# Eighteen additions and subtractions on VectorE, moved one by one between blocks of matmuls

## The reference

```
ua = einsum(ya * silu(ga), w_up_a);  ub, uc in the same way
gates = sigmoid(gm)                  # gm = h @ w_in[:, GM:], 3 x 1024 columns
merged = gates[0] * ua + gates[1] * ub + gates[2] * uc
x = x + merged @ w_o
```

## Time and profile before

| | |
|---|---|
| time, median of 3 runs | 1227.82 us (1226.7 to 1228.06) |
| profiled execution, its own time | 1227.92 us |
| its span from first to last instruction | 1225.8 us |
| PE busy | 1209.8 us, 99% of the span |
| DVE, ACT, POOL busy | 58%, 50%, 58% of the span |
| mean granted clock of TensorE | 0.997 of full speed |

### The profile page before, as it was taken

How to read it: one execution, slowest core, us unless ns; L and a number is a source line. 1 busy time by engine, 2 the same in 40 slices (tenths; PEclk the granted TensorE clock), 3 DMA queues, 4 the chain that set the end, 5 groups by cost and what they waited for, 6 DMA issues and landing times.

```text
span 1225.8 us, 18317 instructions
## 1 busy us (share of the span) xinstructions
PE 1209.8 (99%) x6667; PEld 991.0 (81%) x6667; DVE 711.2 (58%) x1235; ACT 607.9 (50%) x1176; POOL 705.5 (58%) x538
## 2 busy tenths in 40 slices
PE   9999999999998999999999999999999999999997
PEld 7987777787876899987897777878888888889886
DVE  5554427757657777745597555434454445966224
ACT  6365535676633344455645665544444444333544
POOL 8673233263368776856384557446555655886842
PEclk9999999999999999999999999999999999999999
DMA  6332222222222333354142123333333332334332
GB/s 240 106 88 85 60 64 58 60 70 73 59 70 77 95 104 95 105 188 112 52 118 61 46 73 88 103 86 96 92 89 104 96 89 82 103 92 120 107 86 69
DMA packets 62432, 112.22 MB, mean 92 GB/s; under 512 B 6856, under 2 KB 11464, under 8 KB 62344
## 3 DMA queue, kind: packets, MB, share of 16 engines
q1 hardware_dynamic: 62200, 111.06, 31.7%
q10 hardware_dynamic: 144, 0.00, 0.0%
HBM read 108.87 MB, written 2.16 MB: 91 GB/s over the span
## 4 chain that ended last, share of the span: by engine, by line
PE 91%; DVE 5%; ACT 1%; POOL 1%; issue 1%; DMA 0%; SPq 0%; DVEq 0%; POOLq 0%; ACTq 0%
PE pb L1093 22%; PE pb L1094 22%; PE pb L1096 21%; PE pb L1146 3%; PE pb L1148 3%; PE pb L1147 3%; PE pb L1302 2%; DVE t7s L2034 2%; PE pb L1278 2%; PE pb L1155 2%; PE pb L1245 1%; PE pb L1216 1%; PE pb L1218 1%; PE pb L1217 1%; PE pb L1199 1%; PE pb L1197 1%
## 5 line engine op out<-in xcount | busy, mean ns | idle before, releaser
L2650 POOL TENSOR_TENSOR wlo<-raw,whi 128x512 fp32r<-128x512 f32 (+2 forms) x384 | 522.1, 1379 | 331.0 <-ACT whi L1495 330.0
L1093 PE MATMUL pb<-HH,whi 128*128 128x512 f32 x856 | 345.6, 404 | 1.0 <-DVE th L1971 1.0
L1094 PE MATMUL pb<-HL,whi 128*128 128x512 f32 x856 | 338.5, 395 | 0.0
L1096 PE MATMUL pb<-HH,wlo 128*128 128x512 f32 x856 | 337.5, 394 | 0.0
L1495 ACT ACTIVATE whi<-raw 128x512 fp32r<-128x512 f32 (+2 forms) x384 | 226.0, 615 | 105.1 <-PE pb L1096 54.7
L1093 PEld LDWEIGHTS pb<-HH,whi 128*128 128x128 f32 x856 | 161.3, 188 | 43.6 <-issue 4.6
L1094 PEld LDWEIGHTS pb<-HL,whi 128*128 128x128 f32 x856 | 161.1, 188 | 38.0 <-issue 2.9
L1096 PEld LDWEIGHTS pb<-HH,wlo 128*128 128x128 f32 x856 | 160.9, 188 | 37.5
L1959 DVE TENSOR_TENSOR pb<-pb,rff 128x512 f32<-128x512 f32 x44 | 30.8, 700 | 124.0 <-PE pb L1096 117.6
L1604 ACT ACTIVATE P<-P,stat 128x256 f32<-128x256 f32 (+3 forms) x96 | 50.6, 528 | 78.5 <-DVE stat L2212 56.1
L2650 POOL TENSOR_TENSOR fl<-cv,fh 128x512 fp32r<-128x512 f32 x22 | 28.9, 1315 | 86.4 <-ACT fh L1880 86.4
(11 more groups left out here) (459 smaller groups left out, 2526.0 us busy)
## 6 DMA issues: line engine op xcount, KB each, us to landing
raw<-in_wall SPq DMA_DIRECT2D x368, 256.0 KB, 2.8
raw<-in_wall SPq DMA_DIRECT2D x8, 260.0 KB, 3.0
X<-in_xT SPq DMA_DIRECT2D x8, 256.0 KB, 5.1
X<-in_xT SPq DMA_DIRECT2D x2, 1024.0 KB, 7.4
outT<-PP SPq DMA_DIRECT2D x8, 256.0 KB, 2.4
raw<-in_wall SPq DMA_DIRECT2D x10, 192.0 KB, 2.4
raw<-in_wall SPq DMA_DIRECT2D x9, 128.0 KB, 2.5
cst<-in_cst SPq DMA_DIRECT2D x1, 832.0 KB, 7.3
```

The costliest lines, as they stand in the source:

```text
L1093: pe.do.matmul(b, hi, xh[k], start=start, stop=False, skip_group_check=tile[0] == "down")
L1094: pe.do.matmul(b, hi, xl[k], start=False, stop=False, skip_group_check=tile[0] == "down")
L1096: m = pe.do.matmul(b, lo, xh[k], start=False, stop=stop, skip_group_check=tile[0] == "down")
L2650: g.do.tensor_tensor(lo, x, hi.bitcast(F32), ALU.subtract).then_inc(*up(name, point))
```

## The change

Sets 0, 1 and 2 are no longer issued as runs. Their single instructions (`t_piece`, i = 0 to 5) and then the set's `t_parts` go into a list, `extra`, from which `slot` takes one at blocks 1 and 5 of a tile. Set 0 is put in ahead of the gate tiles of C, set 1 ahead of the early `gm` tiles, set 2 after gate tile B0. The 18 DVE instructions, 3 of ACT and 6 of POOL are the same ones as before, in other places; PE and SP keep their rows. `t_sums` stays for set 3 and for the second block.

```diff
@@ slot
     def slot(self, i):
         if i in (3, 7):
             self.step()
+        elif i in (1, 5) and self.extra:
+            self.add(*self.extra.pop(0))
@@ stages
+        def pieces(kp):
+            self.extra += [("t_piece", kp, i) for i in range(6)] + [("t_parts", 0, kp)]
+
+        pieces(0)
         for t in range(4):
             gate("gateC", "yC", t)
+        pieces(1)
         add("masks_in")
         for d in range(3):
             for j in range(3):
                 gm(d, j)
         for t in range(4):
             gate("gateA", "yA", t)
-            if t in (1, 3):
-                add("t_sums", 0, t // 2)
-            if t == 2:
-                add("t_parts", 0, 0)
         for t in range(4):
             gate("gateB", "yB", t)
-            if t < 2:
-                add(("t_parts", "t_sums")[t], 0, 1 + t)
+            if t == 0:
+                pieces(2)
         while self.background:
             self.step()
-        add("t_parts", 0, 2)
+        while self.extra:
+            add(*self.extra.pop(0))
@@ vector
+            def t_piece(kp, i):
+                x11, x12, x21, x22 = (TS7[kp][:, H * n:H * n + H] for n in range(4))
+                v.wait_ge(*at("values", *[("C", 7, 3), ("A", 3, 3), ("B", 7, 3)][kp:kp + 1]))
+                if kp == 2:
+                    v.wait_ge(*at("yA", 3))
+                if i < 2:
+                    n = kp + 4 * i
+                    v.wait_ge(*at("x_lo", n))
+                    v.wait_ge(*at("x_hi", n))
+                    dst, one, two, op = TS7[kp][:, T * i:T * i + T], hh[n].bitcast(F32), hl[n].bitcast(F32), ALU.add
+                else:
+                    v.wait_ge(*last("v_t7"))
+                    dst, one, two = ((x11, x12, x11), (x12, x22, x12), (x22, x22, x11), (x21, x21, x22))[i - 2]
+                    op = ALU.subtract
+                v.do.tensor_tensor(dst, one, two, op).then_inc(*up("v_t7", *[("t_raw", 0, kp)] * (i == 5)))
```

More of the change, by code:

```diff
@@ L192, in __init__ @@
         self.slot_of, self.slot_user, self.slot_before, self.slots = {}, {}, {}, 0
+        self.extra = []
         self.background, self.heads, self.gates, self.ticks = [], [], [], 0
@@ L2633, in half_out @@
                         mul(PP[d][:, c], PP[d][:, c], r, ("final", d, half))
-            follow({"begin": begin, "split": split, "t_sums": t_sums, "product7": product7, "first": first, "square": square,
+            follow({"begin": begin, "split": split, "t_piece": t_piece, "t_sums": t_sums, "product7": product7, "first": first, "square": square,
                     "lambda": lam_dots, "norm1": norm1, "kC_out": kc_out,
```

## The result

The changed kernel takes 1230.08 us (median of 11 runs, 1229.48 to 1231.03), the kernel before 1227.62 (11 runs beside it, 1226.47 to 1228.25). The ratio is 1.0025 with a 95% interval of 1.0017 to 1.0032: a loss of 2.5 us where 1.05 was forecast. The profiled execution has a span of 1227.8 us, 2.0 more than before.

What follows compares the result with a forecast made beforehand. PE bounds the kernel, working 1209.8 of 1225.8 us. Added 0.68 + 0.5 + 3.7 + 1.57 = 6.45 us, taken away 5.40, so 1227.82 + 1.05 = 1228.9 us; range 1223.4 to 1231.0 us, forecast's own 1227.5 to 1230.3.

Steps and rivals of the forecast that it cites:

- What is taken away: Gates of B: PE's waits for th (1.17 us) and yBlo (2.66) and the slow clock (1.57) go, 5.40 us.
- C0 and C1: Gate tiles of C: pieces ahead of score reads make PE wait, 0.68 us in C0 and 0.5 in C1.
- The third gm tile: PE waits 3.7 us for a late read of B's scores, then loses 1.57 us to a slow clock.
- The 1.0 us by which A's last head ends late: Before the third gm tile: ACT's splitting of set 0 (0.3) and set 0's pieces delay A's end 1.0 us.
- The two pieces ahead of the first read: Set 1's pieces before B's first score read, both at the high price beside POOL: 3.18 us, less 0.85 idleness.
- The pieces ahead of the second read: Set 1's next two pieces, before the score read at 280.95: 1.8 us, less 1.42 of DVE idleness.
- The clock: After the long wait at the third gm tile PE's clock falls to 0.50, losing 1.57 us.
- the rule on POOL: POOL holds up DVE instructions with two SBUF inputs or in 2-port mode; every piece exposed, bank reads not.
- Hidden pieces: Rival: pieces mostly run alone, costing 1.1 us, so 4.3 us are gained: 1223.5 us; chance 0.20.
- A wait without the slow clock: Rival: DVE 1 to 3 us late at the second B step, PE stays at 2.4 GHz: 1225.8 us; chance 0.22.
- The other side: Rival: at the second B step PE waits 5.4 us and the clock falls, 3.05 lost: 1230.9 us; chance 0.12.
- the change doesn't do what it says: Rival: B's gates are late for another reason, only the 1.17 us wait goes: 1233.1 us; chance 0.04.

Runs made afterwards that it cites:

- set 1 alone: Against the kernel before, only set 1 taken apart into pieces, ahead of the gm tiles; sets 0 and 2 stay whole runs behind A1 and B1: 1225.29 us, ratio 0.9984.
- set 0 alone: Against the kernel before, only set 0 taken apart into pieces, in C; sets 1 and 2 stay whole runs behind A3 and B1: 1225.27 us, ratio 0.9984.
- parts of set 0 later: Against the changed kernel, the parts of set 0 (ACT's t7h, two t7l on POOL) come behind gate tile A1 instead of C3: 1227.76 us.
- the last kernel: Against the kernel before, only the parts of set 0 moved, behind the last gate of B in place of A2: 1225.88 us, ratio 0.9987.

## Why the prediction was right, and where its sizes were off

**What is taken away: right, 5.6 us against 5.40.** Both waits and the slow clock are gone, and the kernel with all pieces behind gates shows that the sum can be had whole. But the reason given, that the set in front of each gate makes it late, was too narrow. With set 0 or set 1 alone out of the row, runs remain ahead of B0 or B2 and make next to no wait (0.3 us), and with all three runs in place the wait for `th` goes when the parts of set 0 are moved. In these kernels a run makes little or no wait where the gate ahead of it is in time; runs and their parts in a row pass their delays on. That did not enter the sum, since the change takes all three away.

**C0 and C1: 0.57 + 0.71 = 1.28 us against 0.68 + 0.5 = 1.18.** Both are near the reckoning. The piece in C0 ran alone, the one in C1 beside POOL's `wlo` took 1.79.

**The third gm tile: the term that was too small.** The wait was put at 3.7 us and the clock at 1.57, 5.27 together; they took 6.28. That PE would wait here for a score read, and that the clock would fall, came as forecast; the terms from which the size of the wait was summed don't hold one by one:

- The 1.0 us by which A's last head ends late is right: 272.71 - 270.42 is 2.29, less PE's own 1.28. But ACT's `t7h`, for which the prediction counted 0.3 of it, has no share. With the parts of set 0 moved away the lateness is the same, and with set 1 alone there is none (`qA` starts 10.67 us ahead of the transposes, as before); it is the pieces of set 0 themselves.
- The two pieces ahead of the first read took 2.05 + 1.40 = 3.45 us against 3.18. They would have been dear without set 0 as well (1.77 + 1.44 with set 1 alone).
- Not in the sum at all: the masks `B`, two DVE instructions that were there before. The prediction cost `t7l`'s delay of POOL's `wlo` at nothing, because the weights are split ahead; PE indeed waits for no `wlo` from C0 on. But a later `wlo` falls on other DVE work: the pair of masks took 2.68 us in place of 1.58, and 0.48 where POOL was free. With set 0 alone they took 2.66 beside the same three `wlo`, so the pieces of set 1 aren't needed for it. Against the run with the parts of set 0 later, the masks are 2.2 us longer and the two pieces 0.2, while `qA`, which falls on POOL's `CAST` and not on a `wlo`, is 0.7 shorter (0.76 against 1.46): together the 1.7 us. The Trainium skill names two kinds of VectorE work that GpSimd can hold up, two SBUF inputs and a 2-port mode (GPSIMD Engine Reference, section 8, Key points). The prediction applied the first to the pieces alone. The masks have one input; which mode they run in no row shows, but their times, 0.48 to 2.68 with POOL's work, agree with the page's second kind.
- The pieces ahead of the second read were overrated (0.84 us against 1.8), and a normalizing and a 128x1 sum beside POOL's next `wlo` (1.36 and 1.21 us) made up for it. Here the size came out for the wrong reason: the interval between the two reads grew by 7.17 - 6.71 = 0.46 us, and 1.8 - 1.42 = 0.38 was reckoned.
- The clock: it fell as forecast. Reckoned as in the prediction, at 0.23 each, the eight slow spacings lost 1.72 us against 1.57 (1.60 against the same eight of before, 283.81 - 281.85 = 1.96); the transposes ahead of them ran at 1.2 GHz too, some 0.2 to 0.3 more.

In sum 1.28 - 1.18 + 6.28 - 5.27 = 1.1 us more was lost than reckoned, and 5.6 - 5.4 = 0.2 more gained: a net loss of 2.0 us in the profiled executions in place of 1.05. That 2.0 is still near 1.05 is in part luck: what was too much for the pieces ahead of the second read stood against a normalizing and a sum that were left out, and the masks, left out too, against a shorter `qA` (0.76, before 1.47).

**Two readings of the prediction that don't hold.** The row given for the rule on POOL, `th<-th,pb` at 371.51 with 0.68, doesn't test it, since POOL stood idle from 370.86 to 373.67. A row that does is the same instruction of gate tile A3: at 361.47 it took 0.69 beside POOL's `t7l` (from 360.30, two in 2.56), while `th<-th,qA` behind it, with both inputs in SBUF, took 1.20. And the forecast's own range doesn't follow from its bounds: a wait of 3 with C0 and C1 at their lowest gives 1228.1, not 1227.5, and a wait of 4.5 with C0 and C1 at their highest 1231.1, not 1230.3.

**The rivals.** Hidden pieces fell: those of set 1 were dear where they counted. A wait without the slow clock fell for the change, but it is what set 1 alone gives (1.53 us, clock at 1.00). The other side, with a wait of 5.4, was too high in its wait; the time came nearest to it all the same, 1230.08 against 1230.9 (1228.9 was forecast). That the change doesn't do what it says fell with the list of waits. The forecast itself was no difference within 0.2%. The measured loss of 0.25%, with an interval of 0.17 to 0.32, lies clear of no difference; whether it is over 0.2% the interval leaves open. The time is 0.3 us above the forecast's 1228 to 1229.8.

## What to carry to other kernels

A stall that a long run of instructions seems to cause may need several runs in a row: take one of them out first, and see how many have to go. When single operations are strewn between steps, look at what each now precedes (a read that frees a bank is the worst neighbour) and at which engine shares its time; here the same pieces behind gate instructions cost nothing and ahead of score reads some 7 us with the slow clock. An instruction moved on POOL is to be costed by the DVE work that POOL's later queue will fall on, old instructions included, not only by who waits for its result; and one moved on ACT by what stands behind it in ACT's queue.

## What the runs showed of the hardware

- PE's clock fell to 1.2 GHz around waits of 2.49 us (before), 2.55 (parts of set 0 later) and 4.06 us (the change), and stayed at 2.4 behind waits of 1.0, 1.53 and 1.6. In the change it was already down while PE stood still.
- Small VectorE instructions are held up by GpSimd as well: a 128x1 sum that takes 0.15 us alone took 1.21 where POOL's `wlo` ran (284.51 in the change), and the pair of 128x256 masks went from 0.48 to 2.68, more in proportion than the 128x256 differences (0.42 to 1.40).
- A VectorE instruction with two SBUF inputs isn't always the one that waits: `th<-th,qA` took 1.20 us beside POOL's work before and 0.69 in the last kernel, where the two `wlo` beside it took 3.01 in place of about 2.56.
- In some profiled executions PE waits at about 88 us for a DMA of `decay_qB`, 0.2 to 1.0 us, ahead of everything that was edited; in those of before and of the change it doesn't. In the last kernel PE is 0.5 us late from the start on, for a `wlo` at 9 us. Differences of spans under 1 us are read with that in mind.
